# Weight stream in five slots of eight atoms instead of four slots of ten

## The chip, the core and the metric

One core of one Trainium2 chip runs the kernel. The metric is the device time of one execution in microseconds, from the first to the last instruction on the core and the little that lies around them. Runs of the kernel before took 1916.69, 1922.51 and 1923.26 us, median 1922.51 us.

## The reference

256 tokens of width 1024 in float32 go through two models, one after the other, in one launch. Cut to what matters:

```
for i in range(2):                                   # first block, two layers
    z = rmsnorm(x, mix_norm[i]) @ w_in[i]            # 1024 x 6312 of weights
    u, gl, cq, ckv_kr, fq, fk, fv, fl, g = split(z)
    y = [rglru(u, gl) @ w_br_a[i], mla(cq, ckv_kr) @ w_br_b[i], fox(fq, fk, fv, fl) @ w_br_c[i]]
    x = x + (sum(sigmoid(g_b) * y_b for b in range(3))) @ w_o[i]
    hf = rmsnorm(x, ffn_norm[i]) @ w_gate_up[i]
    x = x + (silu(hf[:, :2816]) * hf[:, 2816:]) @ w_down[i]
    x = x + sigmoid(rmsnorm(x, ple_norm[i]) @ w_ple_gate[i]) * (p[i] @ w_ple[i])
x = rmsnorm(x, final_norm)
for i in range(2):                                   # second block: pooling layer, attention layer
    shifts, scales, gates = split(silu(c) @ ada_w[i] + ada_b[i], 6)     # modulation
    x = x + gate1 * mix_i(modulate(rms_norm(x)))     # pool_mix, then attention over context and tokens
    x = x + gate2 * (square(relu(modulate(rms_norm(x)) @ w1[i])) @ w2[i])
return rms_norm(x, final_g)
```

mla and fox are softmax attention with 8 heads over 256 tokens, rglru is a linear recurrence with gates of 64x64 blocks. In its layer 0 the second block also carries 256 tokens of context, so there a product has 512 columns instead of 256.

## The kernel before

**Weights as one stream.** Every weight that is multiplied once is cut into atoms of 128x128 numbers and packed into one array in the order of use: 1218 atoms for each layer of the first block, 1232 for the second block, 3668 in all. A chunk is `CHUNK_ATOMS` (10) consecutive atoms, 640 KB. The stream holds 367 such chunks, called splits, and among them 96 chunks of modulation weights (`ada`, two for each of 48 modulation tiles). An ada chunk holds 8 atoms in the room of 10. `chunk_plan` writes the order of the 463 chunks (`ORDER`) out by hand.

**Four steps for each split chunk.** (1) SyncE issues its transfer into `raw[index % RING]` (L831, loop L850 to L852); the transfer of chunk c+RING waits until chunk c of the order is free. A split is free once GpSimd is done with it (`lo_ready`), an ada chunk once TensorE has multiplied it (`ada_used`). SyncE waits in order, so one chunk that isn't free holds back all later transfers. (2) ScalarE rounds the chunk into `whi[n % RING]` (`split`, L1301 to L1307). It waits for the landing and for `slots_used`, which TensorE raises when it opens a chunk: split n may be written when split n-3 is opened (`FREE_SLOTS` 3). (3) GpSimd writes the rest, raw minus whi, into `wlo[n % RING]` (`lo_parts`, L862 to L871). It does this in one instruction over 1280 columns, or, for the chunks in `SHORT_PIECES` (80, those of each layer of the first block from its first tile to the end of attention), in four of 320 columns; `lo_ready` comes with the last. (4) TensorE multiplies three times for each atom (`product`, L903 to L914: whi by the high part, whi by the low part, wlo by the high part). At the first atom of a chunk it waits for `lo_ready` (`weights`, L884 to L893).

**ScalarE runs ahead by plan.** ScalarE also squares, applies tanh and exp, and rounds activations, all in one program order. `keep_ahead(t)` (L1384, `split_ahead` L1313) does all splits up to `REACH[t]` before ScalarE turns to tile t. `chunk_reach` (L184 to L202) sets the reach: `AHEAD` (3) chunks of the order beyond the tile's last one, then more as long as they are ada chunks or splits less than `SLOTS_AHEAD` (3) beyond those needed. If the chunk at the reach hasn't landed, ScalarE stands, and with it all of its later work.

**Order of tiles.** In a layer of the first block: head (`u`, `gl`, `cq`, `ckv`, `kr`, norms `ss`, small products `wa`, `wx`, then `fv`, `vm`, `kn`, `qn`, `qr`, `rotq`), 16 steps of attention with two filling tiles each (`fl`, `fq`, `fk`, `g`, `y`), the other gates and branches, `wo`, the feed-forward, `pg`/`pp`. In attention step n ScalarE moves the turned probabilities of step n-1 (L1422), does two exps (L1413), then `keep_ahead` and the work of both filling tiles; after step 7 it writes the decay mask of the second attention (L1431). In the head ScalarE squares the tile ckv (L1480) for the norm `ss` that TensorE does at L987. At `qn 0` it rounds the result of the recurrence (L1505), for which VectorE waits before it scales `qr`; only then can TensorE do `rotq` (L1004). In the second block, layer 1, ScalarE squares every q tile (L1697) behind `ahead2(("q", j))`, and TensorE takes it at L1218.

## Time and profile before

| | |
|---|---|
| runs | 1916.69, 1922.51, 1923.26 us |
| profiled execution | 1923.36 us, span 1921.5 us |
| granted TensorE clock, mean | 0.963 |
| TensorE matmul | 1795.2 us busy, 93% |
| GpSimd | 1131.5 us, 59% |
| ScalarE | 868.5 us, 45% |
| VectorE | 834.1 us, 43% |
| DMA, transfers of the stream | 463, 46.4% of 16 engines' span |
| chain that ended last | PE 76%, DVE 8%, POOL 4%, ACT 3%, DMA 3%, issue 3% |

In the profile PE is TensorE's matmuls, PEld its weight loads, DVE VectorE, ACT ScalarE, POOL GpSimd, SP SyncE. A row of a timeline gives start and length in us, engine, line, operation and tiles; in square brackets the idle time before it and what ended it. "PEclk" is the clock that TensorE was granted, as a share of 2.4 GHz: 1.00 is that level and 0.50 is 1.2 GHz; a value between is a mean over time at both.

### The profile page before, as it was taken

The numbers are of one execution on the slowest core, as the hardware profiler recorded it, in microseconds if no ns is written. First come the engines' busy times: TensorE is split into PE (matmuls) and PEld (weight loads), VectorE is DVE, ScalarE is ACT, GpSimd is POOL, SyncE is SP. The second block draws the span as 40 slices with busy tenths as digits, with TensorE's granted clock in tenths as the row PEclk, the third lists the DMA queues.
The fourth block names the chain that finished last, engine by engine and source line by source line (L and its number), as shares of the span: only waits on it lengthen the run. The fifth ranks groups of instructions, "written<-read, shape, count | busy, mean of one in ns | idle before, by whom it ended". The sixth has DMA issues, their size and how long they took to land.

```text
span 1921.5 us, 32487 instructions
## 1 busy us (share of the span) xinstructions
PE 1795.2 (93%) x13080; PEld 1630.0 (85%) x13080; DVE 834.1 (43%) x1970; ACT 868.5 (45%) x1364; POOL 1131.5 (59%) x611
## 2 busy tenths in 40 slices
PE   6889999999998899999999879999999889889997
PEld 5878899999998788999999757777787677679997
DVE  7677435313365775443334852121212445542223
ACT  5535546444665355464446753222323333454443
POOL 5666568778786665778887314343433323147884
PEclk9889999999998999999999979999999889989999
DMA  6453355655464534656555224433445433125552
GB/s 244 144 212 114 124 208 176 239 179 180 164 219 141 203 124 137 235 177 222 180 190 193 97 96 164 151 137 137 151 165 205 178 142 114 33 83 175 182 180 90
DMA packets 70167, 311.51 MB, mean 162 GB/s; under 512 B 7680, under 2 KB 9984, under 8 KB 69760
## 3 DMA queue, kind: packets, MB, share of 16 engines
q1 hardware_dynamic: 68400, 306.47, 46.4%
q10 hardware_dynamic: 1616, 2.95, 0.5%
q8 instruction: 104, 1.70, 0.4%
q14 instruction: 47, 0.39, 0.1%
HBM read 308.34 MB, written 1.05 MB: 161 GB/s over the span
## 4 chain that ended last, share of the span: by engine, by line
PE 76%; DVE 8%; POOL 4%; ACT 3%; DMA 3%; issue 3%; DVEq 2%; ACTq 0%; SPq 0%
PE bank L909 23%; PE bank L913 22%; PE bank L912 22%; POOL wlo L869 4%; DMA raw<-in_stream 3%; PE bank L924 2%; DVE split_acts L1756 1%; ACT whi L1306 1%; PE bank L932 1%; PE bank L1076 1%; PE bank L1106 1%; PE bank L1090 1%; DVE acts L2334 0%; ACT bank L1351 0%; PE bank L1238 0%
## 5 line engine op out<-in xcount | busy, mean ns | idle before, releaser
L869 POOL TENSOR_TENSOR wlo<-raw,whi 128x320 fp32r<-128x320 f32 (+1 forms) x607 | 1131.3, 1888 | 769.0 <-ACT whi L1306 768.2
L909 PE MATMUL bank<-split_acts,whi 128*128 128x256 f32 (+1 forms) x3540 | 1086.0, 307 | 53.3 <-DVE split_acts L1756 31.9
L912 PE MATMUL bank<-split_acts,whi 128*128 128x256 f32 (+1 forms) x3540 | 1068.8, 302 | 0.0
L913 PE MATMUL bank<-split_acts,wlo 128*128 128x256 f32 (+1 forms) x3540 | 1068.3, 302 | 0.0
L909 PEld LDWEIGHTS bank<-split_acts,whi 128*128 128x128 f32 x3540 | 685.2, 194 | 110.5 <-issue 48.6
L913 PEld LDWEIGHTS bank<-split_acts,wlo 128*128 128x128 f32 x3540 | 686.4, 194 | 22.0
L912 PEld LDWEIGHTS bank<-split_acts,whi 128*128 128x128 f32 x3540 | 687.0, 194 | 20.9
L1306 ACT ACTIVATE whi<-raw 128x1280 fp32r<-128x1280 f32 x367 | 464.3, 1268 | 510.8 <-PE bank L909 253.5
L2387 DVE SCALAR_TENSOR_TENSOR acts<-bank,acts 128x256 f32<-128x256 f32 x104 | 47.4, 482 | 230.8 <-PE bank L913 230.8
L2401 DVE TENSOR_SCALAR acts<-bank 128x512 f32<-128x512 f32 (+1 forms) x64 | 35.7, 558 | 212.3 <-PE bank L913 212.3
L1756 DVE TENSOR_TENSOR split_acts<-bank,split_acts 128x256 fp32r<-128x256 f32 (+1 forms) x204 | 94.4, 463 | 53.4 <-ACT split_acts L1447 24.3
L1629 ACT ACTIVATE bank<-acts 128x512 f32<-128x512 f32 (+1 forms) x64 | 31.5, 493 | 101.2 <-DVE acts L2401 101.2
L2070 DVE TENSOR_TENSOR bank<-bank,acts 128x256 f32<-128x256 f32 x44 | 19.0, 432 | 98.7 <-PE bank L913 98.7
L1413 ACT ACTIVATE acts<-acts 128x128 f32<-128x128 f32 (+1 forms) x64 | 28.6, 448 | 68.4 <-DVE acts L1973 68.4
L924 PE MATMUL bank<-raw,acts 128*32 128x256 f32 x768 | 55.7, 411 | 4.2 <-DVE acts L1935 3.6
L1447 ACT ACTIVATE split_acts<-bank 128x256 fp32r<-128x256 f32 x44 | 16.8, 382 | 69.1 <-DVE bank L2075 69.1
L2031 DVE TENSOR_TENSOR acts<-bank,acts 128x256 f32<-128x256 f32 x48 | 20.4, 424 | 54.2 <-PE bank L913 52.8
L2061 DVE TENSOR_TENSOR acts<-bank,acts 128x256 f32<-128x256 f32 x32 | 13.6, 425 | 67.4 <-PE bank L913 67.4
L1438 ACT ACTIVATE acts<-acts 128x256 f32<-128x256 f32 x48 | 24.2, 504 | 38.2 <-DVE acts L2031 38.1
L924 PEld LDWEIGHTS bank<-raw,acts 128*32 128x32 f32 x768 | 21.1, 114 | 23.4 <-issue 8.2
L1351 ACT ACTIVATE bank<-acts 128x256 f32<-128x256 f32 x48 | 27.2, 566 | 25.4 <-DVE acts L2360 24.8
L1756 DVE TENSOR_TENSOR split_acts<-acts,split_acts 128x256 fp32r<-128x256 f32 (+2 forms) x44 | 32.1, 733 | 8.7 <-ACT split_acts L1740 4.5
(265 smaller groups left out, 1562.9 us busy)
## 6 DMA issues: line engine op xcount, KB each, us to landing
raw<-in_stream SPq DMA_DIRECT2D x463, 640.0 KB, 3.9
acts<-in_x SPq DMA_DIRECT2D x1, 1024.0 KB, 6.0
acts<-in_ctx ACTq DMA_DIRECT2D x1, 1024.0 KB, 7.8
acts<-in_const ACTq DMA_DIRECT2D x1, 1024.0 KB, 5.2
out<-acts SPq DMA_DIRECT2D x8, 128.0 KB, 2.1
acts<-in_const SPq DMA_DIRECT2D x1, 708.0 KB, 8.4
acts<-in_p ACTq DMA_DIRECT2D x2, 256.0 KB, 4.0
acts<-in_const ACTq DMA_DIRECT2D x1, 320.0 KB, 3.1
```

The costliest lines, as they stand in the source:

```text
L869: last = nc.gpsimd.tensor_tensor(wlo[slot][:, cols], raw[source][:, cols], whi[slot][:, cols].bitcast(F32), ALU.subtract)
L909: first = nc.tensor.matmul(out_ap, w_hi, hi_act(k), start=(k == 0), stop=False)
L912: nc.tensor.matmul(out_ap, w_hi, lo_act(k), start=False, stop=False)
L913: last = nc.tensor.matmul(out_ap, w_lo, hi_act(k), start=False, stop=(k == k_tiles - 1))
L924: last = nc.tensor.matmul(b[32 * strip:32 * strip + 32, 0:256], silu_c[:, 2 * k:2 * k + 32], raw[c % RING][:, strip * 256:(strip + 1) * 25 ...
L1306: sc.activation(whi[n % RING][:, :], raw[source % RING][:, :], ACT.Copy).then_inc(hi_ready, 1)
L1351: last = sc.activation(dst(t, s), side(tmp, t % 2, s), ACT.Identity, scale=gain_col(l, i, t, s), bias=mod_col(l, SH1 if i == 0 else SH2, t ...
L1413: sc.activation(tile(pr, u % 2)[:, 0:nk], tile(lg, u % 2)[:, 0:nk], ACT.Exp, scale=-1.0, bias=nmax[u % 2], accum_out=rsum[u % 2]).then_inc ...
L1629: sc.activation(hid_home[j % 3][:, a], tile(tmp, j % 2, 512)[:, a], ACT.Square)
L1756: return v.tensor_tensor(lo, value, hi.bitcast(F32), ALU.subtract)
L2387: last = v.scalar_tensor_tensor(out=side(h, n, s), in0=src, scalar=col(s), in1=side(h, n, s), op0=ALU.mult, op1=ALU.add)
L2401: v.tensor_scalar(tile(tmp, j % 2, 512)[:, a], b[:, 0:w], 0.0, None, ALU.max)\
```

## The change

Five constants. A chunk holds 8 atoms (512 KB), and raw, whi and wlo have five slots each, which take the same memory as before (3 x 4 x 1280 and 3 x 5 x 1024 columns). Both distances of running ahead go from 3 to 4 chunks, and so does the number of slots that are free at the start. All that the constants feed is worked out anew: the packing of the stream, `ORDER`, `REACH`, and the pieces of GpSimd, which are 1024 columns or four of 256. An ada chunk now fills its slot.

```diff
-CHUNK_ATOMS = 10
-RING = 4
+CHUNK_ATOMS = 8
+RING = 5
 CH = CHUNK_ATOMS * P
-AHEAD = 3
-SLOTS_AHEAD = 3
+AHEAD = 4
+SLOTS_AHEAD = 4
...
 FREE_BANKS = N_BANKS
-FREE_SLOTS = 3
+FREE_SLOTS = 4
```

## Rows read from the trace of the kernel before

**Rows 1.** Waits, whole trace: engine and line waited for, us in total, times, longest.

```profile
ACT whi L1306 <- PE bank L909: 253.5, 131, 7.0
ACT whi L1306 <- DMA raw<-in_stream: 240.0, 62, 11.8
```

**Rows 2.** Busy us (and count) of each engine in stretches, then PEclk, DMA share, GB/s.

```profile
core 0: us, PE busy (x) PEld busy (x) DVE busy (x) ACT busy (x) POOL busy (x), PEclk, DMA share, GB/s
112.00:129.00 17.00, 13.61 (x84) 11.59 (x84) 9.54 (x29) 6.58 (x10) 8.24 (x11) 0.70 0.64 229
450.00:500.00 50.00, 50.00 (x419) 50.00 (x419) 17.22 (x42) 25.06 (x37) 41.51 (x15) 1.00 0.56 185
638.00:653.00 15.00, 13.08 (x112) 11.68 (x111) 9.35 (x29) 5.82 (x9) 9.44 (x12) 1.00 0.83 295
1552.00:1555.00 3.00, 3.00 (x26) 2.95 (x25) 0.00 (x0) 0.00 (x0) 0.00 (x0) 1.00 0.99 401
```

**Rows 3.** Groups of instructions: GpSimd whole trace by form, ScalarE's rounding: count, busy, mean ns.

```profile
L869 POOL TENSOR_TENSOR wlo<-raw,whi 128x1280 fp32r<-128x1280 f32 x287 | 845.7, 2957 | 616.9 <-ACT whi L1306 616.3
L869 POOL TENSOR_TENSOR wlo<-raw,whi 128x320 fp32r<-128x320 f32 x320 | 285.6, 928 | 152.0 <-ACT whi L1306 151.9
L1306 ACT ACTIVATE whi<-raw 128x1280 fp32r<-128x1280 f32 x367 | 464.3, 1268 | 510.8 <-PE bank L909 253.5 <-DMA raw<-in_stream 240.0 <-PE bank L1235 16.7
L1447 ACT ACTIVATE split_acts<-bank 128x256 fp32r<-128x256 f32 x44 | 16.8, 382 | 69.1 <-DVE bank L2075 69.1
```

**Rows 4.** The same groups, GpSimd between 24 and 65 us.

```profile
L869 POOL TENSOR_TENSOR wlo<-raw,whi 128x320 fp32r<-128x320 f32 x41 | 39.5, 1005 | 11.9 <-ACT whi L1306 11.9
```

**Rows 5.** Transfers: tiles, queue, count, KB each, median us from issue to landing.

```profile
raw<-in_stream SPq DMA_DIRECT2D x463, 640.0 KB, 3.9
out<-acts SPq DMA_DIRECT2D x8, 128.0 KB, 2.1
```

**Rows 6.** Timelines, layer 0, head: GpSimd from 37 us, ScalarE at 68, TensorE at 71.

```profile
37.46 30.77 POOL L869 TENSOR_TENSOR wlo<-raw,whi 128x320 fp32r<-128x320 f32 x32 [1.54 <-ACT whi L1306]
...
68.84 1.27 ACT L1306 ACTIVATE whi<-raw 128x1280 fp32r<-128x1280 f32 x1 [6.92 <-DMA raw<-in_stream]
...
71.67 2.07 PE L987 MATMUL bank<-acts 128*128 128x256 f32 x4 [3.46 <-DVE acts L1936]
```

**Rows 7.** Timelines, layer 0, before rotq: ScalarE, VectorE, TensorE; then TensorE in layer 1.

```profile
106.44 1.07 PE L924 MATMUL bank<-raw,acts 128*32 128x256 f32 x16
...
114.17 1.27 ACT L1306 ACTIVATE whi<-raw 128x1280 fp32r<-128x1280 f32 x1 [6.16 <-DMA raw<-in_stream]
115.77 0.88 DVE L1756 TENSOR_TENSOR split_acts<-acts,split_acts 128x256 fp32r<-128x256 f32 x1 [3.09 <-ACT split_acts L1505]
117.14 0.67 PE L1004 MATMUL bank<-acts 128*128 128x256 f32 x2 [1.76 <-DVE acts L1929]
...
644.50 0.67 PE L1004 MATMUL bank<-acts 128*128 128x256 f32 x2 [0.29 <-issue]
```

**Rows 8.** Timelines, layer 0, attention step 7: ScalarE, then TensorE.

```profile
184.14 2.41 ACT L1306 ACTIVATE whi<-raw 128x1280 fp32r<-128x1280 f32 x2
...
187.50 0.80 PE L1076 MATMUL bank<-acts 64*128 64x128 f32 x4 [2.44 <-ACT acts L1431]
```

**Rows 9.** Timelines, layer 1, head: ScalarE, then TensorE.

```profile
595.29 1.27 ACT L1306 ACTIVATE whi<-raw 128x1280 fp32r<-128x1280 f32 x1 [8.71 <-DMA raw<-in_stream]
...
598.12 1.93 PE L924 MATMUL bank<-raw,acts 128*32 128x256 f32 x16 [3.57 <-DVE acts L1935]
```

**Rows 10.** Timelines, second block, q tiles: SyncE, ScalarE, TensorE.

```profile
1549.58 2.03 SPq L831 DMA_DIRECT2D raw<-in_stream  x4
...
1557.80 1.27 ACT L1306 ACTIVATE whi<-raw 128x1280 fp32r<-128x1280 f32 x1 [8.00 <-DMA raw<-in_stream]
...
1559.48 0.98 PE L1218 MATMUL bank<-acts 128*128 128x1 f32 x4 [2.52 <-ACT acts L1697]
...
1571.98 0.58 PE L1218 MATMUL bank<-acts 128*128 128x1 f32 x4 [0.61 <-ACT acts L1697]
```

## The prediction

> **What bounds the kernel now.** I first read the stretches. Between 450 and 500 us TensorE is busy throughout, with 419 matmuls at full clock [rows 2]. That is 0.119 us each, 0.36 us for the three of an atom, 2.9 us for 8 atoms and 3.6 us for 10. This is the normal state. There no chunk size can help, and an extra wait costs nothing, because the chunk is ready long before TensorE opens it. So I looked for the places where TensorE stands or runs at the low clock behind the stream. The waits show ScalarE standing 240.0 us for landings and 253.5 us until TensorE opens a chunk [rows 1]. Most of that is harmless idle time. It costs where ScalarE's next instruction is one that TensorE needs. Such places I found by following TensorE's gaps back in the timelines: 71.67 us [rows 6], 117.14 us [rows 7], 187.50 us [rows 8], 598.12 us [rows 9], 1559.48 and 1571.98 us [rows 10]. Behind all of them stands a split, L1306. The other large gaps are norms and softmax maxima, which the change doesn't touch.
>
> A second limit shows in the heads of the two layers: 32 pieces of GpSimd without a pause in 30.77 us [rows 6], one every 0.96 us. Four make a chunk of 10 atoms, 3.85 us, while TensorE needs 3.6. There GpSimd is the bound.
>
> **Prices of the parts.**
>
> *GpSimd.* A piece of 320 columns takes 928 ns and one of 1280 takes 2957 [rows 3], so a column costs 2.11 ns and a piece 252 ns apart from its columns. A piece of 256 columns should take 793 ns, one of 1024 2416 ns. The heads and attentions now have 99 x 4 = 396 pieces instead of 320. In the crowded stretch, where a piece takes 1005 ns [rows 4] and follows every 0.96 us, I get 0.25 + 0.8 x 0.71 = 0.82 us, so 3.28 us for 8 atoms, 0.410 us an atom instead of 0.385. Bounds: 0.8 x 0.96 = 0.77 us (all of it goes with the columns) and 0.96 us (none does). I take 0.82, from the two lengths of the same instruction.
>
> *ScalarE.* A split takes 1268 ns and the same rounding of 256 columns 382 ns [rows 3], so 1024 columns take 1.05 us. 459 of these come to 480 us instead of 464; the 16 us are spread over an engine that is 45% busy, and cost nothing except where they stand ahead of a needed instruction. There a split is now 0.22 us shorter.
>
> *Transfers.* 640 KB land 3.9 us after their issue, 128 KB after 2.1 [rows 5], so 512 KB land after 3.45, a gain of 0.45 us wherever one transfer alone is waited for; bounds 0 and 0.8 (in proportion). In a burst the bytes count: at 401 GB/s [rows 2] each 128 KB that is no longer ahead gives back 0.33 us. There are 555 transfers instead of 463 but 4% fewer bytes, as ada chunks no longer carry two empty atoms. On SyncE, 92 more issues lie among waits of many us: nothing.
>
> *TensorE.* 92 more waits for `lo_ready` on a steady stretch: nothing. 32 atoms are rounded ahead instead of 30.
>
> The Trainium skill speaks against smaller transfers ("DMA: Bandwidth & Descriptors", Bandwidth: "Batch DMAs to ≥1 MiB for ≥75% of peak"). An estimate by its fixed part of about 2.0 us and 436 GB/s gives 3.5 and 3.2 us, so a single waited transfer would gain 0.3 us instead of 0.45. No run here has shown 512 KB yet; what the sum would be without any gain stands under the rivals.
>
> **The sum, place by place.**
>
> 1. *Layer 0, ckv* [rows 6]. ScalarE stands 6.92 us until 68.84 for split 13, whose slot is freed by split 11 on GpSimd at 64.9. By the new plan it waits for split 16, freed by split 13, the atoms up to 112 instead of 120. GpSimd starts both at 24.6 us: before 10 chunks of 3.85 and 1.54 us of idle time [rows 6] end at 64.8; now 12 chunks of 3.28 end at 64.0. The idle time goes because the slot that it waits for is freed a chunk earlier. With 0.8 there, 0.45 for the transfer and 0.22 for the split: -1.5 us.
> 2. *Layer 0, qn 0* [rows 7]. Split 20 comes at 114.17, L1505 follows, VectorE has stood 3.09 us for it, TensorE stands 1.76. Now the chunk is split 25. Its transfer can go as soon as ada chunks 8 and 9 are multiplied (106.44 to 107.5), third in a burst; I place it at 112.6, 1.6 us earlier. Layer 1 shows the same place without that wait: a gap of 0.29 us, and full clock from 638 to 653, against 0.70 from 112 to 129 [rows 2]. Half of the clock's part is my guess: 1.6 + 1.4 = -3.0 us, between 0 and -4.5.
> 3. *Layer 1, qn 0.* Here a wait is added: split 177 needs the slot of ada chunk 29, which TensorE multiplies just ahead, while before split 141 needed only GpSimd. The landing comes 4 us after the multiplication. Behind it on ScalarE stands L1505, for which VectorE and rotq wait. I count +0.3, between 0 and +4.5, what layer 0 has today.
> 4. *Layer 0, attention step 7* [rows 8]. Two splits in a row, 2.41 us, stand ahead of the decay mask and the move, and TensorE stands 2.44. By the new reach only one is due there (splits 40 and 41 instead of 32 and 33, the first already done a tile earlier): -1.4 us. The low clock around it should shorten by one 3.4 us piece at half speed: -1.7. Together -3.1, between 0 and -4.5.
> 5. *Layer 1, ckv* [rows 9]. GpSimd's higher price over 70 atoms costs 1.8; 2 atoms less to wait for give 0.8, transfer and split 0.7, an earlier burst 0.8. -0.5 us, between -3 and +2.
> 6. *q tiles* [rows 10]. Four transfers in 2.03 us follow the multiplication of an ada tile; the third is waited for. Three times 128 KB less is -1.0, the split -0.2; at the next ada tile two transfers and the split -0.9, of a gap of 0.61 that caps it, rounded with the clock to -1.0. Together -2.2 us.
> 7. *Layer 0, other attention steps.* Five filling pairs start at atom 186, and the chunk to be opened now opens 6 atoms into its tile, before 2.4 on average. ScalarE goes on later; its next work is due after the second tile. Cover: the rest of the step. I count +0.6, between 0 and +3.
>
> Sum: -1.5 - 3.0 + 0.3 - 3.1 - 0.5 - 2.2 + 0.6 = -9.4 us. Against the profiled execution's 1923.4 us (its span and 1.9 around it, 0.9 above the median of the runs) that is **1914.0 us**.
>
> **Rivals.** *GpSimd takes over.* If a piece of 256 columns follows as slowly as one of 320 (0.96 us), a chunk of 8 takes 3.85, against TensorE's 2.9. Place 1 then ends 12 x 0.57 = 6.8 us later than I have it, layer 1's head 8 or 9 chunks x 0.57 = 5 later, and the norms behind pass it on whole; places 2 and 4 keep about half. 1914 + 12 + 3 = 1929, up to 1935. It decides from a piece of about 0.91 us on, where the gains are eaten. For it: crowded pieces are 77 ns above the mean [rows 3, 4], and that part may hang on the piece. Against: four times the columns cost 3.2 times as much [rows 3], so most of a piece goes with its columns.
>
> *The stream's wait moves.* The waits leave ScalarE, but VectorE or the ada tiles are late next: place 3 at +4.5, place 7 at +3, nothing from the clock in 2 and 4. 1914 + 4.2 + 2.4 + 3.1 = 1924. For it: in order behind one ada chunk SyncE holds back everything, and the plan puts more of these right before needed splits. Against: in places 1, 2, 4 the new plan waits for earlier events.
>
> *A transfer of 512 KB lands no sooner.* Then 1, 5 and 6 lose 0.45, 0.45 and 1.9: 1917.
>
> *The clock comes back in full.* Low-clock stretches stand at four of the six places; at half speed 66 to 84 and 592 to 614 would give 3 us each, and 2 and 4 their whole 4.5: 1904.
>
> **How the numbers follow.** Forecast (1909 to 1919) 0.40; 512 KB no gain 0.10; wait moves 0.15; GpSimd takes over 0.20; clock in full 0.15. The measurement can tell about 0.5%, 9.6 us, from no change: below 1912.9 is faster, above 1932.1 slower. Of the forecast's 0.40, 0.22 lies below 1912.9, as its centre is next to it; with the clock's 0.15 faster is 0.37. Slower: half of GpSimd's 0.20 and a quarter of the moved wait's 0.15, where both price each other up, 0.14. Same: 0.49. The range takes in the clock case's centre and most of GpSimd's: 1902 to 1930.
>
> **What would show it.** Right: GpSimd's pieces near 0.8 us, TensorE's matmul L987 near 70 us in layer 0, no long idle time before L1004, one split ahead of L1431 in step 7, third transfer of the q tiles landed a microsecond sooner, TensorE's total idle time lower by some 6 us. Wrong: pieces at 0.95 and TensorE idle behind L869 between 28 and 65 us; VectorE standing for L1505 in layer 1; or low-clock stretches that begin somewhere else and undo the sum, since a gap of 2 to 3 us decides over each.

## The result

The changed kernel takes 1908.1 us (median of 10 runs, 1902.9 to 1912.2), the kernel before, run beside it, 1919.8 us (10 runs, 1915.2 to 1926.2). The ratio is 0.994, 95% interval 0.9925 to 0.9954, so it is faster by 0.6%. The forecast was 1914.0 with a range from 1902 to 1930. The time is inside it, but 5.9 us below the forecast, and on the side of "faster by over 0.5%", to which I had given 0.37. Of these 5.9 us, 3.6 are the starting point: I subtracted 9.4 us from 1923.4, while the kernel before has its median at 1919.8. The gain itself was 11.7 us against 9.4. In the runs further below, one execution of the kernel before, of 5995.4 us, is left out of the ratios.

The profiled executions differ by more than the medians: the span went from 1921.5 to 1905.7 us, 15.8 us, against 11.7 between the medians. What follows splits up the 15.8. It is one execution of each kernel, and one can lie 5 us off its median (run 2 below: profiled at 1911.4 us, median 1916.2), so a row of the tables below that moves by 1 or 2 us shows little by itself.

Waits of the changed kernel, whole trace (us in total, times, longest), to be read against [rows 1]:

```profile
ACT whi L1306 <- PE bank L909: 348.3, 246, 6.6
ACT whi L1306 <- DMA raw<-in_stream: 187.5, 63, 13.4
```

ScalarE now stands less for landings (187.5 us, before 240.0) and more until TensorE opens a chunk (348.3, before 253.5). That alone says little, as most of both is harmless. The groups and the transfers answer [rows 3] to [rows 5]: GpSimd's two forms over the whole trace, then between 24 and 65 us, then the rounding, then the transfers (count, KB each, median us to landing):

```profile
L869 POOL TENSOR_TENSOR wlo<-raw,whi 128x1024 fp32r<-128x1024 f32 x360 | 862.3, 2402 | 601.2 <-ACT whi L1306 601.0
L869 POOL TENSOR_TENSOR wlo<-raw,whi 128x256 fp32r<-128x256 f32 x396 | 297.6, 788 | 123.3 <-ACT whi L1306 123.2
...
L869 POOL TENSOR_TENSOR wlo<-raw,whi 128x256 fp32r<-128x256 f32 x52 | 41.4, 835 | 10.3 <-ACT whi L1306 10.3
...
L1306 ACT ACTIVATE whi<-raw 128x1024 fp32r<-128x1024 f32 x459 | 482.7, 1055 | 551.8 <-PE bank L909 348.3 <-DMA raw<-in_stream 187.5 <-PE bank L1235 14.6
...
raw<-in_stream SPq DMA_DIRECT2D x555, 512.0 KB, 3.8
```

The prices of GpSimd and ScalarE are as forecast: 788 ns (793), 2402 ns (2416), 1055 ns (1050). In the crowded head 52 pieces take 41.4 us, one every 0.80 us (0.82). The transfer's median is 3.8 us where I had 3.45; the part on the prediction tells why.

The stretches answer [rows 2]; the last one here is the q tiles, whose counterpart of before is given under it:

```profile
core 0: us, PE busy (x) PEld busy (x) DVE busy (x) ACT busy (x) POOL busy (x), PEclk, DMA share, GB/s
112.00:129.00 17.00, 14.06 (x101) 11.83 (x101) 12.02 (x31) 8.10 (x13) 11.67 (x16) 0.80 0.52 184
450.00:500.00 50.00, 50.00 (x419) 50.00 (x419) 17.09 (x40) 27.04 (x41) 41.10 (x18) 1.00 0.55 180
1544.70:1570.80 26.10, 23.41 (x194) 19.94 (x195) 15.41 (x40) 9.54 (x19) 7.10 (x3) 1.00 0.56 203
```

```profile
1558.00:1584.00 26.00, 21.30 (x122) 16.51 (x123) 13.39 (x34) 7.45 (x15) 5.79 (x2) 0.74 0.34 120
```

The steady stretch is as it was: 50.00 us of 50 busy, 419 matmuls. The q tiles ran at a mean granted clock of 0.74 before, that is with two spells at the lower level, 1.2 GHz, and run at the full 2.4 GHz now. The two stretches are of one length but not of one amount of work (194 and 122 matmuls); the table below goes by the work.

**Where the 15.8 us are.** The weight matmuls of a trace (L909, L1016, L1170, L1235), taken in order, give the time at which TensorE first multiplies with each atom of the stream. All kernels here use the same 3668 atoms in the same order, so the difference of these times says how far one is ahead of another at each point. This is the time of the changed kernel minus that of before, with the experiments that are told below beside it (us; "cut" is SLOTS_AHEAD one lower; in order of the columns these are runs 1, 3, 4, 6, 9 and 10):

| atom (place) | before, at | changed | 8 x 5, cut | 8 x 4, dist. 3 | 8 x 5, dist. 3 | 10 x 4, dist. 2 | 10 x 4, cut | 8 x 5, dist. 2 |
|---|---|---|---|---|---|---|---|---|
| 111 | 65.9 | -0.4 | +0.4 | +0.7 | -1.6 | -0.1 | -1.0 | +2.7 |
| 112 (behind place 1) | 74.6 | -2.2 | -4.1 | -0.1 | -6.1 | -4.6 | -5.6 | -1.9 |
| 185 (ahead of place 2) | 113.9 | -1.9 | -2.7 | +2.4 | -2.8 | +2.2 | +1.3 | +6.9 |
| 258 (behind it) | 159.4 | -3.9 | -6.1 | -1.1 | -6.7 | -1.2 | -2.3 | +3.5 |
| 310 (behind places 4, 7) | 193.8 | -5.1 | -7.9 | -2.8 | -8.3 | -2.4 | -3.5 | +1.3 |
| 900 | 430.8 | -3.8 | -6.7 | -1.6 | -7.9 | -1.3 | -3.5 | +1.7 |
| 1300 (ahead of place 5) | 582.0 | -5.2 | -7.2 | -0.9 | -8.5 | +4.5 | -2.7 | +8.4 |
| 1330 (behind it) | 603.3 | -8.6 | -11.8 | -2.7 | -12.8 | +0.1 | -5.6 | +2.7 |
| 1410 (behind place 3) | 651.9 | -8.6 | -10.0 | -1.9 | -11.2 | +6.0 | -5.2 | +8.5 |
| 2100 | 949.1 | -9.9 | -12.6 | -4.3 | -13.6 | +10.0 | -4.7 | +6.6 |
| 2451 | 1089.1 | -2.5 | -14.1 | -3.4 | -12.5 | +10.0 | -4.6 | +10.5 |
| 3011 (ahead of place 6) | 1556.4 | -4.1 | -15.2 | -5.5 | -15.1 | +7.5 | -6.8 | +12.1 |
| 3030 (behind it) | 1583.1 | -13.3 | -23.6 | -9.8 | -22.8 | -0.8 | -15.1 | +2.2 |
| 3667 (end) | 1909.4 | -15.8 | -25.6 | -14.1 | -25.8 | -3.5 | -14.8 | +0.5 |

Differences of successive rows are what each place gave. The column of the changed kernel has the forecast's places in it, and one thing that isn't there: 7.4 us are lost between atoms 2100 and 2451.

**The places in the changed kernel's trace.** The timelines (start, length, engine, line, tiles, count, idle time before it and what ended it), in the order of [rows 6] to [rows 10]. Layer 0, head:

```profile
65.22 1.06 ACT L1306 ACTIVATE whi<-raw 128x1024 fp32r<-128x1024 f32 x1 [7.41 <-DMA raw<-in_stream]
...
67.83 1.07 PE L924 MATMUL bank<-raw,acts 128*32 128x256 f32 x16 [1.05 <-DVE acts L1935]
69.44 2.08 PE L987 MATMUL bank<-acts 128*128 128x256 f32 x4 [0.53 <-DVE acts L1936]
```

Before rotq:

```profile
113.58 0.75 DVE L1756 TENSOR_TENSOR split_acts<-acts,split_acts 128x256 fp32r<-128x256 f32 x1 [2.77 <-ACT split_acts L1505]
114.81 0.67 PE L1004 MATMUL bank<-acts 128*128 128x256 f32 x2 [1.31 <-DVE acts L1929]
```

Attention step 7, with one split where there were two:

```profile
179.83 1.04 ACT L1306 ACTIVATE whi<-raw 128x1024 fp32r<-128x1024 f32 x1
179.90 0.85 PE L1090 MATMUL bank<-acts 128*128 128x128 f32 x4 [1.85 <-DVE acts L1984]
182.52 0.80 PE L1076 MATMUL bank<-acts 64*128 64x128 f32 x4 [1.77 <-ACT acts L1431]
```

Ahead of L1090 the kernel before had this:

```profile
184.21 0.85 PE L1090 MATMUL bank<-acts 128*128 128x128 f32 x4 [1.38 <-DVE acts L1984]
```

Layer 1, head:

```profile
586.46 1.06 ACT L1306 ACTIVATE whi<-raw 128x1024 fp32r<-128x1024 f32 x1 [6.12 <-DMA raw<-in_stream]
589.08 1.07 PE L924 MATMUL bank<-raw,acts 128*32 128x256 f32 x16 [0.57 <-DVE acts L1935]
591.70 2.08 PE L987 MATMUL bank<-acts 128*128 128x256 f32 x4 [1.54 <-DVE acts L1936]
```

The q tiles:

```profile
1550.34 1.06 ACT L1306 ACTIVATE whi<-raw 128x1024 fp32r<-128x1024 f32 x1 [4.58 <-DMA raw<-in_stream]
1553.06 0.58 PE L1218 MATMUL bank<-acts 128*128 128x1 f32 x4 [0.25 <-ACT acts L1697]
...
1563.65 0.58 PE L1218 MATMUL bank<-acts 128*128 128x1 f32 x4 [0.50 <-ACT acts L1697]
```

Before, two more gaps stood behind those of [rows 10], which the forecast didn't count:

```profile
1574.29 0.58 PE L1218 MATMUL bank<-acts 128*128 128x1 f32 x4 [1.11 <-ACT acts L1697]
1575.77 1.05 PE L1222 MATMUL bank<-acts 128*128 128x256 f32 x2 [0.90 <-DVE acts L2511]
```

ScalarE still stands for the stream at each of them, but TensorE's gap behind it is smaller: 1.05 and 0.53 us at layer 0's head (3.46 before), 1.31 (1.76), 1.77 (2.44, but 1.85 stands ahead of L1090 where 1.38 stood, so the two together shrank by only 0.2), 0.57 and 1.54 (3.57), 0.25 and 0.50 (2.52 and 0.61).

**The new wait.** It is in layer 1's last step, where the context is modulated (SyncE, GpSimd, then ScalarE, VectorE, TensorE):

```profile
1059.73 9.30 SPq L831 DMA_DIRECT2D raw<-in_stream  x4
...
1063.77 4.91 POOL L869 TENSOR_TENSOR wlo<-raw,whi 128x1024 fp32r<-128x1024 f32 x2 [1.17 <-ACT whi L1306]
...
1072.00 1.06 ACT L1306 ACTIVATE whi<-raw 128x1024 fp32r<-128x1024 f32 x1 [5.41 <-DMA raw<-in_stream]
1072.96 0.58 ACT L1351 ACTIVATE acts<-acts 128x256 f32<-128x256 f32 x1
...
1074.06 1.69 DVE L1756 TENSOR_TENSOR split_acts<-acts,split_acts 128x256 fp32r<-128x256 f32 x1 [5.98 <-ACT split_acts L1365]
...
1077.20 1.19 PE L1152 MATMUL bank<-acts 128*128 128x256 f32 x2 [7.79 <-DVE acts L2298]
```

By the list of chunk work, ScalarE comes here to split 308, the fourth ahead of what is needed, four ada chunks lying between. Its slot is freed by GpSimd's work on split 307, which ends at 1063.77 + 4.91 = 1068.68. SyncE issues at 1069.0, the chunk lands, and ScalarE, which stood for it for 5.41 us, only then gets to L1351 and L1365, for which VectorE has stood 5.98 us. TensorE stands 7.79 us, where it stood 2.27 before:

```profile
1080.38 1.19 PE L1152 MATMUL bank<-acts 128*128 128x256 f32 x2 [2.27 <-DVE acts L2298]
```

Of the 7.4 us that are lost between atoms 2100 and 2451, 5.0 are idle time of TensorE (7.2 before, 12.1 now) and 2.4 longer busy time at a lower clock. The chunk itself isn't needed until much later. So the chunk that costs 7 us is one for which nobody but ScalarE waits.

### The profile page after: what moved, and what is told of

It reads as the page before. It is cut to its first block, busy times and chain, and to the rows that moved or that the text cites. A ratio compares the mean times of both kernels' runs of the same rounds, so it can differ in the third digit from the quotient of the medians.

```text
span 1905.7 us, 32890 instructions
## 1 busy us (share of the span) xinstructions
PE 1785.0 (94%) x13080; PEld 1624.5 (85%) x13080; DVE 821.7 (43%) x1970; ACT 894.0 (47%) x1456; POOL 1160.1 (61%) x760
## 3 DMA queue, kind: packets, MB, share of 16 engines
HBM read 295.89 MB, written 1.05 MB: 156 GB/s over the span
## 4 chain that ended last, share of the span: by engine, by line
PE 80%; DVE 7%; POOL 4%; ACT 3%; issue 2%; DMA 2%; DVEq 2%; ACTq 0%; SPq 0%
PE bank L909 24%; PE bank L912 23%; PE bank L913 23%; POOL wlo L869 4%; DMA raw<-in_stream 2%; PE bank L924 2%; DVE split_acts L1756 1%; PE bank L932 1%; PE bank L1076 1%; PE bank L1106 1%; PE bank L1090 1%; DVE acts L2334 0%; PE bank L1079 0%; ACT whi L1306 0%; PE bank L1016 0%
## 5 line engine op out<-in xcount | busy, mean ns | idle before, releaser
L869 POOL TENSOR_TENSOR wlo<-raw,whi 128x256 fp32r<-128x256 f32 (+1 forms) x756 | 1159.9, 1557 | 724.5 <-ACT whi L1306 724.2
L909 PE MATMUL bank<-split_acts,whi 128*128 128x256 f32 (+1 forms) x3540 | 1084.8, 306 | 50.0 <-DVE split_acts L1756 29.0
L912 PE MATMUL bank<-split_acts,whi 128*128 128x256 f32 (+1 forms) x3540 | 1069.0, 302 | 0.0
L909 PEld LDWEIGHTS bank<-split_acts,whi 128*128 128x128 f32 x3540 | 685.3, 194 | 106.2 <-issue 46.5
L1306 ACT ACTIVATE whi<-raw 128x1024 fp32r<-128x1024 f32 x459 | 482.7, 1055 | 551.8 <-PE bank L909 348.3
L912 PEld LDWEIGHTS bank<-split_acts,whi 128*128 128x128 f32 x3540 | 686.9, 194 | 20.9
L2061 DVE TENSOR_TENSOR acts<-bank,acts 128x256 f32<-128x256 f32 x32 | 13.6, 425 | 66.7 <-PE bank L913 66.7
L1351 ACT ACTIVATE bank<-acts 128x256 f32<-128x256 f32 x48 | 27.2, 566 | 25.5 <-DVE acts L2360 25.0
```

Source lines behind the costliest of these rows:

```text
L869: last = nc.gpsimd.tensor_tensor(wlo[slot][:, cols], raw[source][:, cols], whi[slot][:, cols].bitcast(F32), ALU.subtract)
L909: first = nc.tensor.matmul(out_ap, w_hi, hi_act(k), start=(k == 0), stop=False)
L912: nc.tensor.matmul(out_ap, w_hi, lo_act(k), start=False, stop=False)
L1306: sc.activation(whi[n % RING][:, :], raw[source % RING][:, :], ACT.Copy).then_inc(hi_ready, 1)
L1351: last = sc.activation(dst(t, s), side(tmp, t % 2, s), ACT.Identity, scale=gain_col(l, i, t, s), bias=mod_col(l, SH1 if i == 0 else SH2, t ...
```

## The experiments

The theories, as the expectations name them. PLAN: what counts is for which chunk's landing or slot ScalarE is made to stand ahead of needed work, so the distances AHEAD and SLOTS_AHEAD decide. DEPTH: more atoms ahead, and the fifth slot, bring the gain. SIZE: the smaller chunk brings it, whatever the distances. BYTES: it is the 128 KB less in each transfer. GRAIN and PHASE came up later and are told where they did. In all runs the kernel before, run beside them, had its median between 1919.8 and 1921.2 us.

**1. SLOTS_AHEAD 3 on the changed kernel.**

```
 AHEAD = 4
-SLOTS_AHEAD = 4
+SLOTS_AHEAD = 3
```

SLOTS_AHEAD limits how far a tile's list runs on past ada chunks. Of 637 tiles 199 get a shorter list.

> The changed kernel with SLOTS_AHEAD 3 instead of 4; nothing else. The reach shrinks by one chunk at 199 of 637 tiles, among them pg 7 of layer 1, where it no longer takes in split 308 behind four modulation chunks. Theory PLAN (what moves the time is for which chunk's landing or slot ScalarE is made to stand ahead of work that TensorE needs): in the changed kernel TensorE stood 7.75 us at 1077 us behind that split, in the kernel before 2.24; that goes back to about 2, and the heads gain a little more, as ckv 1 waits for split 15 instead of 16. 5 to 8 us faster than the changed kernel, some 18 us under the kernel before. Rival DEPTH (being further ahead is what helps): one chunk less of reach costs, 2 to 5 us slower than the changed kernel. Rival NEITHER (durations alone matter): the same as the changed kernel within 2 us.

Measured: 1898.7 us, ratio to before 0.990 (0.9872 to 0.9928), 9.4 us below the changed kernel, where PLAN had 5 to 8 below and DEPTH 2 to 5 above. At the same place as above:

```profile
1061.72 1.04 ACT L1306 ACTIVATE whi<-raw 128x1024 fp32r<-128x1024 f32 x1
...
1063.64 0.59 ACT L1351 ACTIVATE acts<-acts 128x256 f32<-128x256 f32 x1
...
1067.56 0.76 PE L1152 MATMUL bank<-acts 128*128 128x256 f32 x1 [0.42 <-DVE acts L2298]
```

One split comes, L1351 follows without a wait, and TensorE stands 0.42 us (PLAN had about 2). The table above shows it too: between atoms 2100 and 2451 this kernel gains 1.5 us on before, the changed one loses 7.4. So the new wait comes from the chunk that was taken in too early; with it the stretch costs 8.9 us more.

**2. Before, with ada transfers cut to their 8 atoms.**

```
-sp.dma_start(raw[slot][:, :], stream[index]).then_inc(raw_in[slot], 16)
+w = ADA_ATOMS * P if ORDER[index][0] == "ada" else CH
+sp.dma_start(raw[slot][:, 0:w], stream[index][:, 0:w]).then_inc(raw_in[slot], 16)
```

> The kernel before, only that the transfer of a modulation chunk carries its 8 atoms and leaves the two empty ones out; four slots of ten otherwise. It takes the fewer bytes of a burst by themselves. Theory PLAN: bytes are a small part, the q tiles (1549 to 1590 us), where bursts of modulation chunks stand ahead of a split, gain 1 to 2 us of the 9 that the change gained there, and the whole 1 to 3 us. Rival BYTES (shorter transfers are what gains): the q tiles gain at least 5 us and the whole 5 to 8.

Measured: 1916.2 us, ratio 0.998 (0.9959 to 1.0001), so the saved bytes are worth 0 to 0.4%. That lies between the theories: by the medians it is 5.0 us, at the lower edge of what BYTES had (5 to 8) and above PLAN's 1 to 3. By the first multiplications it gains 3.6 us between atoms 3011 and 3030, again between BYTES (at least 5) and PLAN (1 to 2); the changed kernel gains 9.2 there. So bytes are a part of the gain, and not shown to be a small one. Its transfers (count, KB, median us to landing):

```profile
raw<-in_stream SPq DMA_DIRECT2D x367, 640.0 KB, 3.9
raw<-in_stream SPq DMA_DIRECT2D x96, 512.0 KB, 4.4
```

The 512 KB ones land later than the 640 KB ones, as many are issued in bursts at the ada tiles. Those of either size that were issued with no other on the way land after 3.49 us (37 of 512 KB) and 3.85 us (170 of 640 KB), in the median. So the median over all holds a good deal of what lies ahead in the queue, and isn't the price of a size.

**3 and 4. The slot by itself: eight atoms, distances 3, with four slots and with five.**

```
 CHUNK_ATOMS = 8
-RING = 5
+RING = 4             (run 3 only)
-AHEAD = 4
-SLOTS_AHEAD = 4
+AHEAD = 3
+SLOTS_AHEAD = 3
-FREE_SLOTS = 4
+FREE_SLOTS = 3       (run 3 only)
```

> Chunks of 8 atoms, but four slots and the distances of the kernel before (3, 3, 3): 24 atoms ahead instead of 30 or 32, and a fifth less memory. It takes the size alone. Theory PLAN: the steady stretches don't notice (margin of 6 us before each chunk), but the slots of raw come free one chunk later, so the crowded heads stand at raw: 5 to 15 us slower than the changed kernel, near the kernel before. Rival SIZE (finer granularity is the gain, the fifth slot is not needed): within 3 us of the changed kernel. Rival DEPTH: clearly slower than the kernel before, by 10 us or more.

> The changed kernel with five slots of eight atoms, but AHEAD 3 and SLOTS_AHEAD 3: ScalarE is told to go on a chunk earlier everywhere, the slots that it may use are the same. Theory PLAN: ScalarE's waits for landings nearly vanish, the places gain like or more than with SLOTS_AHEAD 3 alone, 5 to 12 us faster than the changed kernel, unless the stream then comes too late for TensorE in the crowded heads. Rival DEPTH: 24 atoms of lead are too few, TensorE stands for wlo in heads and attentions, 5 to 20 us slower than the changed kernel.

Measured: four slots 1910.2 us (ratio 0.9953, 0.9938 to 0.9969), five slots 1899.2 us (0.990, 0.987 to 0.9929). The lists of the two differ at only 23 of 637 tiles, so 11 us are the slot's. For four slots I had expected much worse, 5 to 15 us above the changed kernel; it was 2.1 above it, within the 3 us that SIZE had. It takes less memory than the kernel before, 32 atoms in place of 40, and is still some 9 to 11 us faster (by the ratio, by the medians). Five slots at distance 3 came out 8.9 us below the changed kernel, as PLAN had it (5 to 12). Both went against what DEPTH had (four slots 10 us or more above the kernel before, five at distance 3 5 to 20 above the changed one), though the slot, which it names too, is worth 11 us. Layer 0's head, four slots, then five:

```profile
68.93 1.06 ACT L1306 ACTIVATE whi<-raw 128x1024 fp32r<-128x1024 f32 x1 [6.32 <-DMA raw<-in_stream]
...
71.55 2.07 PE L987 MATMUL bank<-acts 128*128 128x256 f32 x4 [2.65 <-DVE acts L1936]
```

```profile
64.09 1.06 ACT L1306 ACTIVATE whi<-raw 128x1024 fp32r<-128x1024 f32 x1 [3.75 <-DMA raw<-in_stream]
...
66.92 1.10 PE L987 MATMUL bank<-acts 128*128 128x256 f32 x4 [0.29 <-DVE acts L1936]
...
raw<-in_stream SPq DMA_DIRECT2D x555, 512.0 KB, 3.4
```

ScalarE asks both times for a chunk at the same distance. With a fifth slot that chunk doesn't have to wait for a slot that GpSimd frees last, and the split comes 4.84 us earlier; 2.3 us of that the kernel was ahead already at atom 111. And here a transfer of 512 KB lands after 3.4 us, in the changed kernel after 3.8. That number doesn't follow slots or list in any simple way: four slots (run 3) have 3.4 too, the changed kernel with SLOTS_AHEAD 3 (run 1) 3.6, and the changed kernel padded (run 8) 3.6 with its list as it was.

**5. Before, with short chunks in five pieces of 256 columns.**

```
-lo_parts(n, 4 if n in SHORT_PIECES else 1)
+lo_parts(n, 5 if n in SHORT_PIECES else 1)
```

> The kernel before, with the low parts of the short chunks in five pieces of 256 columns in place of four of 320: GpSimd's fixed cost by itself. A piece of 256 columns takes 788 ns in the changed kernel, one of 320 took some 920 in the kernel before, so a short chunk costs GpSimd 5 x 788 = 3940 ns in place of 3680, some 0.26 us more in each of about 80 chunks, 20 us of GpSimd's time in all. Cover theory (this lies beside TensorE's work, except where GpSimd is late): 1918 to 1924. Rival (in the crowded stretches GpSimd ends the wait, and each chunk's 0.3 us is paid): 1925 to 1935.

Measured: 1923.1 us, ratio 1.0016 (1.0001 to 1.0032), some 3 us, inside what the cover theory had (1918 to 1924).

```profile
L869 POOL TENSOR_TENSOR wlo<-raw,whi 128x256 fp32r<-128x256 f32 x400 | 299.3, 788 | 140.9 <-ACT whi L1306 140.7
```

A piece costs 788 ns in either kernel, so its price goes with its columns and not with its chunk, and 14 us more of GpSimd's time (299.3 against 285.6) cost 3. The rival "GpSimd takes over" lacked its condition: a piece of 256 columns would have had to cost 0.91 us or more.

**6. Before, with distances 2.**

```
-AHEAD = 3
-SLOTS_AHEAD = 3
+AHEAD = 2
+SLOTS_AHEAD = 2
```

> The kernel before, ten atoms and four slots as they were, with both planned distances 2 in place of 3 (each tile's list of chunk work reaches one chunk less far). Chunks, bytes and pieces are the old ones. PLAN (what counts is for which chunk's landing ScalarE stands ahead of work that is needed sooner, and one slot must be left beyond the distance): the step from the changed kernel to distances 3 gave 9 us (1908.1 to 1898.7 and 1899.2), so here 1905 to 1913, with ScalarE's idle before DMA down from 240 us to under 190. SIZE (the smaller chunk itself brings the gain, whatever the distance): 1917 to 1923, no change. NEITHER (the list is too short, TensorE waits for a chunk that isn't split yet): above 1925.

Measured: 1921.2 us, ratio 1.0011 (0.9997 to 1.0025). PLAN, which had expected 1905 to 1913, missed, although its mark came true: ScalarE's wait for landings fell from 240.0 to 128.8 us. The time is the one that SIZE had (1917 to 1923), but run 9 below takes that support away again.

```profile
ACT whi L1306 <- DMA raw<-in_stream: 128.8, 43, 8.5
...
86.92 5.82 POOL L869 TENSOR_TENSOR wlo<-raw,whi 128x320 fp32r<-128x320 f32 x7 [9.60 <-ACT whi L1306]
...
90.31 0.39 PE L1016 MATMUL bank<-whi,split_acts 128*128 128x256 f32 x1 [2.73 <-POOL wlo L869]
```

The table shows why. At place 1 it gains 4.5 us and at place 6 8.3; but between atoms 112 and 185 it loses 6.8, and between 1330 and 2100 9.9. There ScalarE splits late, GpSimd stands idle for 9.60 us and then TensorE stands for GpSimd. By the waits of the whole trace, TensorE stood for L869 2.4 us in the kernel before, 1.6 in the changed one and 13.4 here. A list that is too short takes from GpSimd what it gives to ScalarE. That isn't all of the loss: of it, 2.7 us fall between atoms 112 and 185 and 2.9 between 1330 and 2100, and the rest there is a lower clock and gaps behind VectorE.

This made a new theory, GRAIN: the right distance in front of the ada chunks lies between 20 and 30 atoms, and only chunks of eight can hit it.

**7 and 8. The boundaries moved: four unused atoms ahead of the stream.**

```
+PAD = 4
...
-ATOMS = DEPTH * LAYER_ATOMS + B2_ATOMS
+ATOMS = DEPTH * LAYER_ATOMS + B2_ATOMS + PAD
...
-atom = 0
+atom = PAD
```

Atom spans and the packed stream are shifted with it. Nothing else of before (run 7) or of the changed kernel (run 8) is altered, except that run 7 comes to one chunk more (368 splits for 367; run 8 stays at 459). This tests PHASE: where the boundaries happen to fall.

> The kernel before with four unused atoms ahead of the stream's first: every tile meets the chunk boundaries 4 atoms later than it did, with sizes, slots and distances as they were. PHASE (a good part of the change's 12 us is where the boundaries happen to fall, above all the 9 us at layer 1's query tiles and the 3 us at its ckv tile): the time moves by 5 us or more, 1908 to 1930. SIZE and PLAN (it lies in the chunk and the distances): 1916 to 1924.

> The changed kernel with the same four unused atoms ahead (half a chunk of 8). PHASE: the time moves by 5 us or more from 1908, and the 7.8 us gap at the 1077 us mark either goes (some 1901) or others of its kind come (1915 and more). SIZE and PLAN: 1904 to 1912, and ahead of the padded kernel before by 8 to 16 us.

Measured: before padded 1917.3 us (ratio to before 0.9988, 0.9976 to 1.0001), changed padded 1910.6 us (0.9954, 0.9936 to 0.9972). Each moved by 2.5 us and in opposite directions. The change is worth 11.7 us unpadded and 1917.3 - 1910.6 = 6.7 us padded. So neither side had it: PHASE expected moves of 5 us or more, and the gap between the two came out below the 8 to 16 us of the other side. Two of many alignments are too few for a mean. The two ratios of the change, 0.9925 to 0.9954 and 0.9936 to 0.9972, overlap, so that 5 of the 12 us depend on alignment is suggested and not shown. The new wait is there in the padded kernel as well:

```profile
1069.36 1.06 ACT L1307 ACTIVATE whi<-raw 128x1024 fp32r<-128x1024 f32 x1 [3.79 <-DMA raw<-in_stream]
...
1074.57 1.19 PE L1153 MATMUL bank<-acts 128*128 128x256 f32 x2 [5.34 <-DVE acts L2299]
```

(its lines are one number higher). So that wait belongs to the distance and not to one boundary.

**9. Before, with SLOTS_AHEAD 2 alone.** The same cut as in run 1, on the old chunks.

```
 AHEAD = 3
-SLOTS_AHEAD = 3
+SLOTS_AHEAD = 2
```

> The kernel before with SLOTS_AHEAD 2 in place of 3 and AHEAD left at 3: ten atoms, four slots. It is to the kernel before what distances (4, 3) are to the changed kernel: only the run-on of a tile's list past the next chunk is cut. Shorter distances alone (2, 2) gave 1921.2: they won some 10 us at the 1080 us mark and at layer 1's query tiles, and lost as much where TensorE then waited for low parts. CUT (the run-on is what makes ScalarE stand ahead of needed work, and cutting it is safe, since GpSimd's chunks come by the first distance): 1906 to 1914, as 1908.1 went to 1898.7. GRAIN (with chunks of ten there is no distance that suits both ends; the cut must lie between 20 and 30 atoms, which only the smaller chunk gives): 1917 to 1923.

Measured: 1909.5 us, ratio 0.9948 (0.9929 to 0.9968). CUT was right, GRAIN in its form "no distance suits chunks of ten" fell, and so did SIZE as the only cause, since the old chunks give as much. One number in the kernel before gives what the change of chunks and slots gave. TensorE stood for L869 6.2 us here, against 13.4 in run 6: AHEAD 3 keeps GpSimd fed where no ada chunk is near. By the table the 11.3 us between the two kernels come mostly between atoms 900 and 2100. One such gap, the one of run 6, remains, and with it the 6.9 us that both lose between atoms 112 and 185:

```profile
89.38 0.39 PE L1016 MATMUL bank<-whi,split_acts 128*128 128x256 f32 x1 [2.70 <-POOL wlo L869]
```

Set together, medians in us:

| | run-on as in the diff | run-on one chunk shorter |
|---|---|---|
| 10 atoms, 4 slots | 1919.8 to 1921.2 | 1909.5 |
| 8 atoms, 5 slots | 1908.1 | 1898.7 |

The two steps add up. The chunks with their slot are worth some 11 us in either column (11.7 and 10.8), the cut 9.4 us in the lower row and 11.1 in the upper (against the 1920.6 of before beside that run).

**10. The changed kernel with distances 2.**

```
-AHEAD = 4
-SLOTS_AHEAD = 4
+AHEAD = 2
+SLOTS_AHEAD = 2
```

> The changed kernel with both distances 2 (16 atoms of reach; five slots and their count as they are). GRAIN: 16 atoms is too short for GpSimd, whose low parts of a chunk of eight take 2.4 us in one piece or 4 x 0.8 in four, and which stands up to 8 us behind in the crowded stretches: TensorE waits for low parts as it did with 20 atoms, 1905 to 1918, slower than distances 3 (1899). PLAN (the less ScalarE stands ahead of needed work the better): 1890 to 1899.

Measured: 1923.1 us, ratio 1.001 (0.9998 to 1.0022), worse than either side had it, though in the direction of GRAIN.

```profile
89.42 6.22 POOL L869 TENSOR_TENSOR wlo<-raw,whi 128x256 fp32r<-128x256 f32 x9 [7.32 <-ACT whi L1306]
...
92.25 0.58 PE L1016 MATMUL bank<-whi,split_acts 128*128 128x256 f32 x1 [4.37 <-POOL wlo L869]
```

GpSimd has stood 7.32 us for a split, and TensorE stands 4.37 for GpSimd. In all it stood for L869 20.3 us. Of the three distances tried with five slots of eight, 3 (24 atoms) is the best: 1923.1 at 2, 1899.2 at 3, 1908.1 at 4.

**11. The cut and the moved boundaries together:** the changed kernel with SLOTS_AHEAD 3 and PAD 4.

> The changed kernel with SLOTS_AHEAD 3 and four unused atoms ahead of the stream: whether the 9 us of that distance hold when the boundaries fall elsewhere. PLAN: they do, 1898 to 1904, against 1910.6 of the changed kernel padded alike. PHASE (the 9 us were one gap at one boundary): 1906 to 1912.

Measured: 1894.8 us, ratio 0.987 (0.9846 to 0.9893), the fastest of all, 13.3 us below the changed kernel. PLAN had 1898 to 1904 and PHASE 1906 to 1912; the time is below both. So the cut holds at another alignment, and by the medians is worth more there, 1910.6 - 1894.8 = 15.8 us. Against the kernel before, padded alike, the kernel with the cut gains 22.5 us, as it does unpadded (22.5). At the place of the new wait:

```profile
1062.99 1.19 PE L1153 MATMUL bank<-acts 128*128 128x256 f32 x2
```

TensorE goes into L1153 without a gap (no bracket in the row).

## Why the prediction was right, and where it wasn't

The sum was -9.4 us, the traces show -15.8. TensorE's busy time, for the same 13080 matmuls, fell by 10.2 us (1795.2 to 1785.0), and its idle time by 5.6 (126.3 to 120.7). The forecast had some 6 us of idle time, and that came out, with the 5.0 us of the new wait against it. The term that it mis-sized is the clock: about 3 us in the sum (1.4 at place 2, 1.7 at place 4), and 10.2 in the traces. Some of that may lie in the two executions that were profiled, as the medians are only 11.7 us apart. By places, from the first table:

| place | forecast | measured |
|---|---|---|
| 1, layer 0 ckv (atoms 111 to 112) | -1.5 | -1.8 |
| 2, layer 0 qn 0 (185 to 258) | -3.0 | -2.0 |
| 4 and 7, layer 0 attention (258 to 310) | -2.5 | -1.2 |
| 5, layer 1 ckv (1300 to 1330) | -0.5 | -3.4 |
| 3, layer 1 qn 0 (1330 to 1410) | +0.3 | 0.0 |
| 6, q tiles (3011 to 3030) | -2.2 | -9.2 |
| layer 1's last step (2100 to 2451) | not there | +7.4 |
| all the rest | 0 | -5.6 |

**The bound.** That the steady stretch can't gain and that every place lies behind a split was right: 50.00 of 50 us before and after, and at the places of the table the time came back behind splits of ScalarE.

**Prices.** GpSimd and ScalarE to within 1%, also in the crowd, 0.80 us for 0.82. So the two lengths of one instruction were enough to price a third. Run 5 confirms the price in the old chunks, and prices GpSimd's extra time: 14 us of it for 3 of the kernel's.

**The transfer.** The median of 3.8 us against the 3.45 forecast looks like the rival by which 512 KB land no sooner. It isn't, once the transfers are sorted by how many earlier ones hadn't landed when they were issued (median us to landing, and how many, from each transfer's issue and landing in the two traces):

| on the way at issue | 640 KB, before | 512 KB, changed |
|---|---|---|
| none | 3.85 (195) | 3.28 (154) |
| one | 3.93 (188) | 3.52 (263) |
| two | 6.33 (57) | 5.20 (76) |
| three | 7.42 (23) | 6.67 (42) |

So a transfer that goes alone gained 0.57 us for the 0.45 forecast, and one behind two others 1.1. The changed kernel has 62 transfers with three or more ahead of them, the kernel before 23, and that lifts its median. The Trainium skill's fixed part plus bandwidth ("DMA: Bandwidth & Descriptors", Anatomy of one DMA), measured there on transfers issued by GpSimd while these are issued by SyncE, gave 3.2 us as an estimate, which agrees with the 3.28; for 640 KB it gave 3.5, and 3.85 were measured. The advice of the Trainium skill to batch to 1 MiB or more (same page, Bandwidth) is about bandwidth, and size over time from issue to landing agrees in its direction, 160 GB/s for 512 KB alone and 170 for 640 KB. But the kernel is faster with the smaller ones, so here that wasn't what decides.

**Places 1 and 2** came close, the second for other reasons than forecast. At 1 the shorter gap is all of it. At 2 the 1.6 us for a sooner landing didn't come: the split lands 7.7 us behind the start of the ada multiplication in both kernels (106.44 to 114.1 before, 104.43 to 112.1 now), TensorE's idle time fell by only 0.45, and the idle time before L1004, which should have gone, is 1.31 us. The clock gave the rest, 1.6 us less busy time between atoms 185 and 258. Its part was named a guess, 1.4, and that was about right: the stretch from 112 to 129 us went from 0.70 to 0.80.

**Places 4 and 7** gave half. One of the two splits ahead of L1431 did go, but in the same step the gap ahead of L1090 grew from 1.38 to 1.85 us, and the low clock didn't get shorter: the mean granted clock is 0.83 in the 20 us around the step in both traces (176 to 196 before, 172 to 192 after). I had counted a gap as saved without asking what the step before it would then wait for.

**Place 3** is the one place where a wait was added on paper. ScalarE did stand for that landing, 7.58 us, but VectorE stood only 0.51 us for L1505 and TensorE not at all: with the landing 4.2 us after the multiplication, the cover was enough.

**Place 5** was taken at -0.5 in a range of -3 to +2, and it gave -3.4, outside it. Between the two atoms TensorE's idle time went from 4.3 to 2.1 us, which is 2.2 of it. The other 1.2 are busy time (16.95 to 15.76), and so the clock, which the forecast left out at this place. The stretch of 26 us around it, before and then after:

```profile
590.00:616.00 26.00, 20.66 (x119) 17.57 (x118) 12.79 (x26) 12.76 (x19) 12.88 (x16) 0.67 0.51 178
```

```profile
582.00:608.00 26.00, 22.41 (x140) 19.98 (x139) 14.04 (x29) 13.13 (x20) 17.42 (x26) 0.74 0.56 195
```

**Place 6** is the largest miss. I gave 2.2 us for a gap of 2.52 and one of 0.61. Between the two atoms TensorE's idle time fell by 3.2 us (5.7 to 2.6), and its busy time, at a clock of 1.00 for 0.74, by 5.9 (20.9 to 15.0). I had hardly counted the clock there, by rounding 0.9 up to 1.0. The rival "the clock comes back in full" looked for it at the heads and at places 2 and 4 and not here (its terms, besides, add up to 1905 and not 1904).

My reason was fewer bytes in the burst, with the split third in it. The traces' single transfers show that in the changed kernel it is second. This is the split that ScalarE stands for at the first of these tiles, by issue and landing:

| kernel | ada chunks ahead in the burst | issue to landing, us |
|---|---|---|
| before (10 x 4) | two | 7.29 |
| before, ada cut (run 2) | two | 5.55 |
| 8 x 4, dist. 3 (run 3) | two | 6.50 |
| changed (8 x 5) | one | 4.39 |

With five slots the first of these ada chunks (90) takes a slot that a split (375) frees, and it is issued 11 us ahead of the burst. With four slots it waits for an ada chunk (88) that TensorE multiplies just before the burst. Runs 1 and 4, with five slots too, have the split second as well, at 4.23 and 4.54 us. So bytes and slot both have a part, 1.7 us by run 2 and 2.1 between run 3 and the changed kernel, and the split landed 2.9 us sooner where I had 1.0. Run 2, with the bytes alone, gets 3.6 us at this place, run 3 4.3, the padded kernel before 5.4 by a shift of boundaries, and runs 6 and 9, which leave chunks and transfers as they were and only shorten the list, 8.3. So unlike edits shorten these gaps, and the clock comes back with them.

**The missing place** cost 7.4 us, and it was the rival "the stream's wait moves" in the flesh, at a place where I hadn't looked. I had checked the new list at the places that stood out in the trace of before. At this place that trace showed two gaps, of 2.3 and 2.6 us, which I put down to norms. The new list should have been read at every tile that has ada chunks behind it. Without this place the change would have been worth 11.7 + 7.4 = 19.1 us; run 1, which takes it away, is 21 to 22.5 us below before.

**All in all** the forecast's -9.4 misses 13.8 us of gain and a loss of 7.4. Of the gain, 8.2 lie at its places (9.9 more than forecast at 5 and 6, 1.7 less at the others) and 5.6 in the rest, in steps of under 3 us that I haven't followed to a cause. That the gain came out as near as it did is in part luck: the two errors have opposite signs. And part of what the change gave may be due to where boundaries fell: with four atoms of padding it is 6.7 us.

**What stays open.** Why smaller chunks are worth 11 us at an equal run-on isn't settled in one cause. Runs 3 and 4 show that a fifth slot does it at equal distances; but four slots of eight, with less memory, are as much ahead of four slots of ten. Those two differ in size and in distance in atoms (24 for 30) at once. Four slots of ten with the cut, 1909.5, equal four slots of eight at 24 atoms, 1910.2, which fits the distance in atoms as the cause there, and the fifth slot as the cause of the rest. But it is only a fit: the two come to the same time by different places (run 9 gains 4.6 us at place 1 and 8.3 at place 6 and loses 6.9 between atoms 112 and 185; run 3 gains 0.8 and 4.3 and loses 2.5). I haven't tried other sizes with both held equal.

## What to carry to other kernels

When work is handed out in order by a list that looks ahead, look at what an engine is made to stand for, and whether somebody needs it: too short a look-ahead starves the next engine in the line, too long a one makes the first stand for a buffer that comes free late, in front of work that is needed now. Measure both distances around the present one before changing the size of the pieces; here one number gave as much as the new chunks and slots together. And pad the stream by part of a chunk, more than once if you can: it gives an idea of how much of a gain belongs to the design and how much to where the boundaries happen to fall.

## What the runs showed of the hardware

- A GpSimd subtraction of 128 x 256 takes 788 ns, of 128 x 320 928, of 128 x 1024 2402 and of 128 x 1280 2957: 2.11 ns a column and some 250 ns apart from that, the same in two kernels.
- A 512 KB transfer that was issued with no other on the way landed after 3.28 us, a 640 KB one after 3.85; with two on the way it was 5.20 and 6.33 us. The median over all 512 KB transfers of a kernel was 3.4 us in one, 3.8 in another and 4.4 in a third.
- TensorE's clock was worth more than the gaps that it fell with: at the q tiles 3.2 us less idle time came with 5.9 us less busy time, the mean granted clock between the same atoms going from 0.74 to 1.00. Over the whole trace the change's idle time fell by 5.6 us and its busy time by 10.2, with the mean clock going from 0.963 to 0.969.
